# A four-layer hybrid decoder on one core: every projection as a float32r product plus a bf16 product of the rests

## The chip, the cores and the metric

The kernel runs on one core of a Trainium2 chip. The metric is the device time of one execution in microseconds. PE is TensorE (PEld its weight loads), DVE is VectorE, ACT is ScalarE, POOL is GpSimd, and SP is the engine that issues the loads from HBM. PSUM is the memory that PE writes, 8 banks of 512 words per partition; SBUF is the large on-chip memory.

## The reference

```python
D_MODEL, SEQ, DEPTH, D_FF, D_RNN, D_INNER = 1024, 512, 4, 2816, 1280, 2048
for i in range(DEPTH):
    hn = _rmsnorm(x, mix_norm[i])
    mix = (_rg_lru_mixer, _ssd_mixer, _swa_mixer, _hgrn2_mixer)[i](hn, ...)
    x = x + mix
    x = x + _conv_ffn(_rmsnorm(x, ffn_norm[i]), ffn_w_up[i], ffn_conv_w[i], ffn_conv_b[i], ffn_w_down[i])

def _rg_lru_mixer(h, ...):                     # mixer 0, "lru"
    proj = h @ w_in                            # 1024 -> 2 x 1280
    xc = _causal_dwconv(xr, conv_w, conv_b)    # 4 taps
    gates = einsum('bsnc,nce->bsne', xb, w_gate) + b_gate      # ten 128 -> 256 products
    a = exp(-8 * sigmoid(r) * softplus(-lam)); u = sqrt(1 - a * a) * (i * xc)
    hs = scan(a, u); return (gelu(gate_branch) * hs) @ w_out   # 1280 -> 1024

def _ssd_mixer(h, ...):   # mixer 1: h @ w_in (1024 -> 5152), 4-tap convolution, chunked scan, norm, @ w_out (2048 -> 1024)
def _swa_mixer(h, ...):   # mixer 2: h @ w_in (1024 -> 1536), windowed attention with sinks, @ w_out (1024 -> 1024)
def _hgrn2_mixer(h, ...): # mixer 3: h @ w_in (1024 -> 4096), gated linear recurrence, norm, gate, @ w_out (1024 -> 1024)

def _conv_ffn(h, w_up, conv_w, conv_b, w_down):
    u = _causal_dwconv(h @ w_up, conv_w, conv_b)               # 1024 -> 2 x 2816, 3 taps
    return (silu(u[..., D_FF:]) * u[..., :D_FF]) @ w_down      # 2816 -> 1024
```

## The kernel before

Activations lie transposed: 128 features on the partitions, the 512 positions along the free axis, so a projection is made of matmuls of 128x128 weights on 128x512 activations. A *panel* holds the weights of one output tile, `w_panel`, in a ring of 4 (`RING`). It is 1024 words wide for 8 inner tiles, up to 1408 for 11. SP loads the panels in a fixed order, each engine's program is written out by hand, and the engines meet through semaphores: `panel_landed` (the DMA), `panel_split` (POOL's part is made), `panel_used` (PE has finished the panel), `banks_free` (DVE has emptied the PSUM bank), `x_split`, `g_split` and `..._y_split` (the activations are ready in two parts).

float32 is emulated by splitting both operands.

- In the four mixers a value is its upper 16 bits (bf16) and a bf16 remainder. PE reads the upper halves of the weights straight from `w_panel`, and POOL makes `w_lo` (L237). `product` (L291, L292, L293) is three bf16 matmuls: high x high, high x low, low x high. The normalised input is `x_hi` and `x_lo`, the mixer's result `g_hi` and `g_lo`.
- In the FFNs a value is `big` (127/128 of it, rounded to float32r) and `rest` (what is left, in float32r as well). ACT makes `w_big` (L270), then POOL makes `w_rest` (L244). `paired` (L311, L312) is two float32r matmuls: big x big and rest x rest; since `big` is scaled, the two together give the product divided by 128, and the reader of PSUM multiplies it back.

An FFN is done in two halves of the inner width: 12 of the 22 up tiles, the first half of the down projection (`dna`, 8 output tiles of 11 inner tiles), the other up tiles, then `dnb`. `g_big` and `g_rest` are rings of 13 tiles.

Mixer 0 (lines 765 to 874) works in ten units. In a unit DVE takes two projection tiles out of PSUM (L824, L827), applies three taps of the convolution (L840), forms the recurrence (L846 to L850, L860, the scan L862) and splits the result (L874). ACT does the first tap (L781), the gates' tanh, exp and tanh (L765 to L773), the square root (L793) and the high part of the result (L795). Mixer 1 has 41 input tiles in four groups of ten; six tiles of a group go through three taps on DVE (L1268), and in the next group's first tiles the scan's products of the previous group are interleaved. Mixer 2 interleaves 12 tiles with 16 attention units, whose exponentials are ACT's (L1871). Mixer 3 interleaves, for each of 8 heads, eight half tiles with eight levels of its recurrence: PE multiplies (L1470), DVE updates (L1619 to L1622, L1632), PE multiplies again. `residual_scalar` and `residual_vector` take each output tile of a projection into the residual stream and prepare the next norm and its splits, tile by tile.

In the trace the stages are: mixer 0 from 0 to 235.7 us, FFN 0 to 478.4, mixer 1 to 922.8, FFN 1 to 1165.5, mixer 2 to 1422.9, FFN 2 to 1665.6, mixer 3 to 2006, FFN 3 to the end. PE's last stretch in each mixer, in which it does little but the output projection, begins at 187, 880, 1390 and 1960 us.

## Time and profile before

| | before |
|---|---|
| median of 3 runs | 2253.49 us (2251.11 to 2255.06) |
| the profiled execution | 2254.03 us, its span 2252.2 us |
| PE busy | 2075.1 us (92%), 9938 matmuls |
| PE weight loads | 1379.8 us (61%) |
| DVE busy | 1333.1 us (59%) |
| ACT busy | 1060.0 us (47%) |
| POOL busy | 919.6 us (41%) |
| granted TensorE clock, mean | 0.966 |
| chain that ended last | PE 71%, DVE 14%, ACT 10%, issue 3%, DMA 1% |

Matmuls overlap each other, so the busy time of a group of them is more than what they add to the time: their starts tell the pace. A granted clock of 1.0 is 2.4 GHz and 0.5 is 1.2 GHz; means lie between.

### The profile page before, as it was taken

What the parts mean: (1) busy time and instruction counts of PE and PEld (TensorE: products, weight loads), DVE (VectorE), ACT (ScalarE), POOL (GpSimd) and SP (SyncE); (2) the same over time, 40 slices, a digit from 0 to 9 for tenths busy, and PEclk for the clock granted to TensorE, in tenths of its full rate; (3) what the DMA queues carried; (4) which work ended last, traced back from release to release, by engine and by line L of the source; (5) the groups of instructions that cost most, each with busy time, mean ns of one, the idle gap of its engine ahead of it and who ended that gap; (6) DMA issues with size and microseconds to landing.
All of it is one profiled execution on the core that took longest, in us unless ns stands there. A gap on an engine that the chain in (4) does not pass through costs nothing.

```text
span 2252.2 us, 26237 instructions
## 1 busy us (share of the span) xinstructions
PE 2075.1 (92%) x9938; PEld 1379.8 (61%) x9938; DVE 1333.1 (59%) x2011; ACT 1060.0 (47%) x1493; POOL 919.6 (41%) x390
## 2 busy tenths in 40 slices
...
GB/s 157 84 67 59 147 168 115 174 84 65 48 66 66 56 58 93 140 158 131 154 110 57 28 19 38 150 162 123 160 93 66 57 57 57 38 131 156 143 141 122
DMA packets 59165, 225.05 MB, mean 100 GB/s; under 512 B 6688, under 2 KB 7072, under 8 KB 58784
## 3 DMA queue, kind: packets, MB, share of 16 engines
...
## 4 chain that ended last, share of the span: by engine, by line
PE 71%; DVE 14%; ACT 10%; issue 3%; DMA 1%; POOL 0%; SPq 0%; DVEq 0%; ACTq 0%; POOLq 0%
PE psum L311 21%; PE psum L312 21%; PE psum L291 7%; PE psum L292 7%; PE psum L293 7%; DVE arena L1268 3%; PE psum L1470 2%; ACT arena L1871 1%; DVE arena L1943 1%; DVE arena L1948 1%; ACT arena L1155 1%; ACT L447 1%; PE psum L1829 1%; DVE arena L1601 1%; ACT arena L1881 1%
## 5 line engine op out<-in xcount | busy, mean ns | idle before, releaser
L244 POOL TENSOR_TENSOR w_rest<-w_panel,w_big 128x1024 fp32r<-128x1024 f32 (+1 forms) x240 | 626.7, 2632 | 350.0 <-ACT w_big L270 332.9
L237 POOL TENSOR_TENSOR w_lo<-w_panel 128x1024 bf16<-128x1024 f32 (+2 forms) x145 | 288.4, 1989 | 961.1 <-DMA w_panel<-in_ssd_in 243.7
L311 PE MATMUL psum<-x_big,w_big 128*128 128x512 f32 x1408 | 550.3, 391 | 0.0
L312 PE MATMUL psum<-x_rest,w_rest 128*128 128x512 f32 x1408 | 547.9, 389 | 0.0
L291 PE MATMUL psum<-x_hi,w_panel 128*128 128x512 bf16 x840 | 331.4, 395 | 22.9 <-DVE x_lo L420 12.4
L292 PE MATMUL psum<-x_lo,w_panel 128*128 128x512 bf16 x840 | 329.9, 393 | 0.0
L270 ACT ACTIVATE w_big<-w_panel 128x1024 fp32r<-128x1024 f32 (+1 forms) x240 | 263.2, 1132 | 140.5 <-PE psum L312 132.7
L293 PE MATMUL psum<-x_hi,w_lo 128*128 128x512 bf16 x840 | 329.2, 392 | 0.0
L311 PEld LDWEIGHTS psum<-x_big,w_big 128*128 128x128 f32 x1408 | 264.3, 188 | 56.6 <-issue 1.0
L312 PEld LDWEIGHTS psum<-x_rest,w_rest 128*128 128x128 f32 x1408 | 264.3, 188 | 55.7 <-issue 1.0
L312 PE MATMUL psum<-g_rest,w_rest 128*128 128x512 f32 x704 | 278.8, 396 | 0.0
L311 PE MATMUL psum<-g_big,w_big 128*128 128x512 f32 x704 | 278.1, 395 | 0.0
L630 DVE SCALAR_TENSOR_TENSOR psum<-ffn_raw,params,psum 128x512 f32<-128x512 f32 x352 | 264.4, 751 | 6.8
L622 DVE TENSOR_TENSOR ffn_raw<-psum,rstd 128x512 f32<-128x512 f32 x176 | 121.7, 692 | 164.3 <-PE psum L312 147.6
L578 ACT ACTIVATE psum<-ffn_raw,params 128x512 f32<-128x512 f32 x176 | 137.4, 782 | 119.2 <-DVE ffn_raw L622 118.8
L291 PEld LDWEIGHTS psum<-x_hi,w_panel 128*128 128x128 bf16 x840 | 86.8, 103 | 129.2 <-issue 44.9
L437 DVE SCALAR_TENSOR_TENSOR x_resid<-psum,x_resid 128x512 f32<-128x512 f32 x64 | 44.0, 688 | 187.8 <-PE psum L312 187.8
L312 PEld LDWEIGHTS psum<-g_rest,w_rest 128*128 128x128 f32 x704 | 132.1, 188 | 32.5
L311 PEld LDWEIGHTS psum<-g_big,w_big 128*128 128x128 f32 x704 | 132.3, 188 | 31.5
L293 PEld LDWEIGHTS psum<-x_hi,w_lo 128*128 128x128 bf16 x840 | 84.9, 101 | 107.0 <-issue 14.3
L292 PEld LDWEIGHTS psum<-x_lo,w_panel 128*128 128x128 bf16 x840 | 85.1, 101 | 102.7 <-issue 25.1
L291 PE MATMUL psum<-g_hi,w_panel 128*128 128x512 bf16 x336 | 130.7, 389 | 9.5 <-DVE g_lo L874 6.1
...
## 6 DMA issues: line engine op xcount, KB each, us to landing
w_panel<-in_upa SPq DMA_DIRECT2D x96, 512.0 KB, 3.5
w_panel<-in_upb SPq DMA_DIRECT2D x80, 512.0 KB, 3.5
...
w_panel<-in_ssd_in SPq DMA_DIRECT2D x41, 512.0 KB, 3.2
w_panel<-in_hgrn_in SPq DMA_DIRECT2D x32, 512.0 KB, 3.2
w_panel<-in_lru_in SPq DMA_DIRECT2D x19, 512.0 KB, 3.5
w_panel<-in_ssd_out SPq DMA_DIRECT2D x16, 512.0 KB, 3.2
```

Of the source, the lines that this page charges most:

```text
L237: pool.tensor_tensor(k.wl[:, slot, lo:words], raw[:, lo:], k.whi(slot, words)[:, lo:], ALU.subtract).then_inc(k.s("panel_split"), 1)
L244: pool.tensor_tensor(k.w2[:, slot, 0:words], raw, k.w1[:, slot, 0:words].bitcast(F32), ALU.subtract).then_inc(k.s("panel_split"), 1)
L270: act.activation(k.w1[:, slot, 0:words], k.w[:, slot, 0:words], ACT.Copy, scale=(SHIFT - 1) / SHIFT).then_inc(k.s("panel_big"), 1)
L291: pe.matmul(out, wh, ah, start=start, stop=False)
L292: pe.matmul(out, wh, al, start=False, stop=False)
L293: return pe.matmul(out, wl, ah, start=False, stop=stop)
L311: pe.matmul(out, w_big, a_big, start=start, stop=False)
L312: return pe.matmul(out, w_rest, a_rest, start=False, stop=stop)
L578: act.activation(out, k.ffn_raw[:, j % 2, half, 2:], ACT.Identity, bias=k.p("ffn_conv_b", j + (l * 2 * FF_T + half * FF_T)), scale=k.p("ff ...
L622: dve.tensor_tensor(k.ffn_raw[:, j % 2, half, 2:], k.ps[:, k.bank(job, i), :], k.rstd[:, :], ALU.mult).then_inc(k.s("banks_free"), 1)
L630: dve.scalar_tensor_tensor(out, k.ffn_raw[:, j % 2, half, tap:tap + S], k.p("ffn_conv_w", j + ((l * 3 + tap) * 2 * FF_T + half * FF_T)), o ...
L1268: dve.scalar_tensor_tensor(place, b.raw[:, i % 2, tap:tap + S], k.p("ssd_conv_w", tap * 24 + ch), place, ALU.mult, ALU.add).then_inc(k.s(" ...
```

## The change

All projections, those of the mixers too, become one float32r matmul on the big parts (L290 of the new kernel) and one bf16 matmul on the rests (L291). `w_rest`, `x_rest` and `g_rest` are bf16 everywhere, and the scale (`SHIFT`) goes from 128 to 512. ACT rounds every panel (`w_big`), in the mixers too: `round_ahead` stands in ACT's program at chosen places and rounds the panels up to four ahead. POOL takes the rest of every panel. SP reloads a ring slot when its panel is split (`panel_split`) in the mixers as well. All panels are at most 1024 words: the output projections are cut into parts of 5, 7 or 8 inner tiles (`OUT_PARTS`), the first parts of the first output tiles ahead of the others (`out_panel`). The FFN keeps its whole inner width of 22 tiles in `g_big` and `g_rest`, so there is one down projection, and the 8 additions to the residual of `dna` go in each FFN. In mixer 0 the convolution, the square of the decay and the result before its split live in PSUM. Mixer 1's normalised results go through PSUM, mixer 3's result too. In all, 1196 triples of bf16 matmuls and 2112 float32r pairs become 3308 mixed pairs.

```diff
-SHIFT = 128.0
+PANEL = DT * P
+SHIFT = 512.0
+OUT_PARTS = {"lru_out": parts((0, 5, 10)), "ssd_out": parts((0, 8, 16)), "swa_out": parts((0, 8)),
+             "hgrn_out": parts((0, 8))}
+OUT_PARTS.update({f"dn{l}": parts((0, 8, 15, 22)) for l in range(DEPTH)})
+OUT_EARLY = {"lru_out": 2, "ssd_out": 4, "swa_out": 2, "hgrn_out": 4, **{f"dn{l}": 2 for l in range(DEPTH)}}
...
+        self.w1 = sb("w_big", [P, RING, PANEL], F32R)
+        self.w2 = sb("w_rest", [P, RING, PANEL], BF16)
+        self.x1 = sb("x_big", [P, DT, S], F32R)
+        self.x2 = sb("x_rest", [P, DT, S], BF16)
...
+def round_until(act, k, last):
+
+    while k.rounded <= min(last, len(PANELS) - 1):
+        n = k.rounded
+        slot, lo, words = n % RING, PANEL // 2 if n == 0 else 0, PANELS[n][2]
         if n >= RING:
+            act.wait_ge(k.s("panel_used"), n - RING + 1)
+        act.wait_ge(k.s(f"panel_landed{slot}"), 16 * (n // RING + 1))
+        act.activation(k.w1[:, slot, lo:words], k.w[:, slot, lo:words], ACT.Copy, scale=(SHIFT - 1) / SHIFT
+                       ).then_inc(k.s("panel_big"), 1)
+        k.rounded += 1
+
+
+def round_ahead(act, k, job, i):
+
+    round_until(act, k, k.panel0[job] + i + RING)
...
-    pe.matmul(out, wh, ah, start=start, stop=False)
-    pe.matmul(out, wh, al, start=False, stop=False)
-    return pe.matmul(out, wl, ah, start=False, stop=stop)
...
+    pe.matmul(out, w_big, a_big, start=start, stop=False)
+    return pe.matmul(out, w_rest, a_rest, start=False, stop=stop)
...
 def residual_scalar(act, k, c, job):
...
+            last = out_panel(job, o, len(OUT_PARTS[job]) - 1)
+            round_ahead(act, k, job, last - 1)
             act.wait_ge(k.s("banks_free"), k.evicted(job, o))
+            round_ahead(act, k, job, last)
...
+    for k0, k1 in OUT_PARTS[job][:-1] + [(OUT_PARTS[job][-1][0], FF_T - 1), (FF_T - 1, FF_T)]:
+        pe.wait_ge(k.s("g_split"), FF_T * l + k1)
+        for o in range(early):
+            out_steps(pe, k, job, o, k0, k1, k.g1, k.g2)
+    for o in range(early, DT):
+        out_steps(pe, k, job, o, 0, FF_T, k.g1, k.g2)
...
-            act.activation(b.conv[:, u, :], b.raw[:, u, 3:], ACT.Identity, bias=k.p("lru_conv_b", j),
+            act.activation(k.ps[:, conv_bank(u), :], b.raw[:, u, 3:], ACT.Identity, bias=k.p("lru_conv_b", j),
                            scale=k.p("lru_conv_w", j + 3 * LRU_T)).then_inc(k.s("lru_biased"), 1)
...
+            round_ahead(act, k, job, 2 * j + 1)
...
+        act.wait_ge(k.s("lru_decay"), j * 3 + 1)
+        act.activation(k.ps[:, 5, :], b.a, ACT.Square).then_inc(k.s("lru_decay"), 1)
...
-            dve.wait_ge(k.s("lru_decay"), r * 2 + 1)
-            dve.tensor_tensor(b.s, b.a, b.a, ALU.mult).then_inc(k.s("lru_s"), 1)
...
+            dve.wait_ge(k.s("lru_decay"), r * 3 + 3)
+            dve.scalar_tensor_tensor(b.s, k.ps[:, 5, :], 1.0, b.th, ALU.add, ALU.mult).then_inc(k.s("lru_s"), 1)
...
@@ ssd_scalar, conv
                            scale=k.p("ssd_conv_w", 3 * 24 + ch)).then_inc(k.s("ssd_biased"), 1)
+            round_ahead(act, k, "ssd_in", ssd_tile(g, i))
             act.wait_ge(k.s("ssd_tapped"), 3 * ci + 3)
```

The first place is ACT's program in one unit of mixer 0. Before the change it has the first tap (L781), the gates' group (L765 to L773), the two copies for the splits, the square root and the high part.

```order
L779 ACTIVATE arena<-arena 128x512
L781 ACTIVATE arena<-arena,params 128x512
L765 ACT_TABLE_LOAD
L765 ACTIVATE arena<-psum,arena 128x512
L768 ACTIVATE arena<-psum,arena 128x512
L772 ACTIVATE arena<-arena 128x512
L773 ACTIVATE arena<-arena 128x512
L787 ACTIVATE arena<-arena 128x512
L789 ACTIVATE arena<-arena 128x512
L793 ACT_TABLE_LOAD
L793 ACTIVATE arena<-arena 128x512
L795 ACTIVATE g_hi<-arena 128x512
```

In the changed kernel the same stretch of ACT reads so (the gates' group is L722 to L732 now).

```order
L738 ACTIVATE arena<-arena 128x512
L742 ACTIVATE psum<-arena,params 128x512
L237 ACTIVATE w_big<-w_panel 128x1024 x2
L722 ACT_TABLE_LOAD
L722 ACTIVATE arena<-psum,arena 128x512
L725 ACTIVATE arena<-psum,arena 128x512
L729 ACTIVATE arena<-arena 128x512
L730 ACTIVATE arena<-arena 128x512
L732 ACTIVATE psum<-arena 128x512
L755 ACTIVATE arena<-arena 128x512
L757 ACTIVATE lru_conv_big<-psum 128x512
L762 ACT_TABLE_LOAD
```

Two roundings of whole panels now stand between the first tap and the gates' group, and the group has one more member, the square.

The second place is ACT in mixer 1, where the exponentials of the previous group's scan (L1175, L1179) and a tile's convolution (first tap L1155, silu L1158) alternate. Before the change:

```order
L1175 ACTIVATE g_lo<-psum 128x384
L1179 ACTIVATE g_hi<-psum 128x512 x2
L1155 ACTIVATE arena<-arena,params 128x512
L1158 ACT_TABLE_LOAD
L1158 ACTIVATE arena<-arena 128x512
L1187 ACTIVATE x_sq<-arena 128x512
```

In the changed kernel (exponentials L1140 and L1144, first tap L1118, silu L1122):

```order
L1140 ACTIVATE arena<-psum 128x384
L1144 ACTIVATE arena<-psum 128x512 x2
L1118 ACTIVATE arena<-arena,params 128x512
L237 ACTIVATE w_big<-w_panel 128x1024
L1122 ACT_TABLE_LOAD
L1122 ACTIVATE arena<-arena 128x512
L1152 ACTIVATE x_sq<-y_plain 128x512
```

A rounding moves in behind each first tap, ahead of the silu's table load. POOL's subtraction for that panel waited for the panel to land, and now waits for this rounding.

## Rows read from the trace of the kernel before

**Rows 1.** First part of the page: engine, busy us, share, instructions.
```profile
PE 2075.1 (92%) x9938; PEld 1379.8 (61%) x9938; DVE 1333.1 (59%) x2011; ACT 1060.0 (47%) x1493; POOL 919.6 (41%) x390
```

**Rows 2.** Chain of waits, whole run, its shares by line.
```profile
by line: PE psum L311 21.5%; PE psum L312 21.5%; PE psum L291 6.7%; PE psum L292 6.6%; PE psum L293 6.6%; issue 3.2%; DVE arena L1268 3.0%; PE psum L1470 2.3%; ACT arena L1871 1.3%; DVE arena L1943 0.9%; DVE arena L1948 0.8%; ACT arena L115
```

**Rows 3.** Busy time: stretch, us, PE, PEld, DVE, ACT, POOL, clock, DMA share, GB/s.
```profile
25.00:187.00 162.00, 129.24 (x546) 55.10 (x544) 139.09 (x182) 87.84 (x119) 45.46 (x21) 0.92 0.20 65
235.70:478.40 242.70, 242.70 (x1059) 198.50 (x1058) 149.00 (x208) 135.62 (x168) 158.27 (x61) 1.00 0.44 146
880.00:922.80 42.80, 42.80 (x200) 19.39 (x199) 9.90 (x16) 11.39 (x17) 17.81 (x9) 1.00 0.33 111
1230.00:1350.00 120.00, 89.77 (x517) 54.37 (x517) 65.31 (x139) 72.12 (x186) 9.46 (x5) 0.92 0.07 23
1390.00:1422.90 32.90, 32.89 (x155) 14.73 (x152) 13.69 (x21) 14.85 (x23) 11.05 (x6) 1.00 0.34 113
1735.00:1960.00 225.00, 202.97 (x1134) 126.47 (x1132) 119.35 (x261) 60.79 (x73) 44.63 (x23) 0.93 0.15 55
```

**Rows 4.** Timeline of PE in three stretches: start, us, engine, line, operation.
```profile
624.66 0.38 PE L293 MATMUL psum<-x_hi,w_lo 128*128 128x512 bf16 x1
...
628.54 0.38 PE L293 MATMUL psum<-x_hi,w_lo 128*128 128x512 bf16 x1
...
249.62 0.39 PE L311 MATMUL psum<-x_big,w_big 128*128 128x512 f32 x1
...
252.79 0.39 PE L311 MATMUL psum<-x_big,w_big 128*128 128x512 f32 x1
...
1159.69 0.40 PE L311 MATMUL psum<-g_big,w_big 128*128 128x512 f32 x1
...
1165.52 0.40 PE L312 MATMUL psum<-g_rest,w_rest 128*128 128x512 f32 x1
```

**Rows 5.** Groups by form; after the bar busy us, mean ns, idle before.
```profile
L244 POOL TENSOR_TENSOR w_rest<-w_panel,w_big 128x1024 fp32r<-128x1024 f32 x176 | 419.1, 2401 | 297.1 <-ACT w_big L270 280.0 <-PE psum L312 17.1
L237 POOL TENSOR_TENSOR w_lo<-w_panel 128x1024 bf16<-128x1024 f32 x136 | 266.9, 1963 | 890.3 <-DMA w_panel<-in_ssd_in 243.7 <-DMA w_panel<-in_hgrn_in 189.9 <-DMA w_panel<-in_swa_out 144.3
...
L270 ACT ACTIVATE w_big<-w_panel 128x1024 fp32r<-128x1024 f32 x176 | 177.1, 1045 | 71.8 <-PE psum L312 63.9 <-DMA w_panel<-in_upa 7.9
```

**Rows 6.** Chain by line: 187:235.7, 585:672, 805:880, 1735:1960, 1960:2006 us.
```profile
by line: PE psum L291 31.4%; PE psum L292 30.9%; PE psum L293 30.1%; DVE arena L862 2.5%; DVE arena L860 1.4%; DVE arena L870 1.4%; DVE g_lo L874 1.4%; ACT g_hi L795 1.3%; issue 0.4%; DVEq L873 0.0%
...
by line: DVE arena L1268 21.4%; issue 6.8%; PE psum L292 6.0%; PE psum L293 6.0%; PE psum L291 6.0%; DVE arena L1342 5.8%; ACT arena L1155 5.5%; ACT L1175 4.4%; DVE g_hi L1322 4.2%; DVE arena L1339 4.0%; DVE arena L1335 3.2%; PE psum L1059 
...
by line: PE psum L291 19.4%; PE psum L292 19.0%; PE psum L293 18.7%; PE psum L1102 8.1%; PE psum L1092 3.6%; PE psum L1059 3.5%; issue 3.0%; PE psum L1037 2.6%; PE psum L1083 2.4%; PE psum L1080 2.4%; PE psum L1078 2.3%; PE psum L1047 2.3%;
...
by line: PE psum L1470 17.7%; PE psum L293 14.8%; PE psum L291 14.8%; PE psum L292 14.8%; DVE arena L1601 5.6%; issue 4.2%; PE psum L1500 2.5%; PE psum L1508 2.4%; DVE arena L1596 2.2%; DVE arena L1658 2.2%; DVE arena L1622 2.1%; DVE arena 
...
by line: PE psum L291 25.5%; PE psum L292 25.1%; PE psum L293 24.9%; DMA w_panel<-in_hgrn_out 6.8%; POOL w_lo L237 4.1%; PE psum L1508 2.4%; PE psum L1470 2.4%; PE psum L1500 2.2%; PE psum L1503 1.5%; PE psum L1492 1.5%; ACT x_sq L1542 1.3%
```

**Rows 7.** Timeline of DVE, ACT and POOL in one unit of mixer 0.
```profile
88.88 0.68 DVE L824 TENSOR_TENSOR arena<-psum,rstd 128x512 f32<-128x512 f32 x1
...
90.20 0.81 ACT L781 ACTIVATE arena<-arena,params 128x512 f32<-128x512 f32 x1
...
93.08 2.32 POOL L237 TENSOR_TENSOR w_lo<-w_panel 128x1024 bf16<-128x1024 f32 x1 [6.13 <-DMA w_panel<-in_lru_in]
...
94.32 1.63 DVE L846 TENSOR_TENSOR arena<-arena 128x512 f32<-128x512 f32 x1 [0.67 <-ACT arena L772]
...
98.80 2.80 DVE L862 TENSOR_TENSOR_SCAN arena<-arena 128x512 f32<-128x512 f32 x1
```

**Rows 8.** Three lines: duration ns min/median/max, first and last start.
```profile
L870 DVE SCALAR_TENSOR_TENSOR arena<-arena x10: 678/680/2389, 54.6 to 188.6; 128x512 f32<-128x512 f32 x10
...
L1268 DVE SCALAR_TENSOR_TENSOR arena<-arena,params x72: 750/752/2432, 515.9 to 801.5; 128x512 f32<-128x512 f32 x72
...
L1601 DVE TENSOR_TENSOR arena<-arena x8: 683/2380/2382, 1680.4 to 1927.6; 128x512 f32<-128x512 f32 x8
```

More of the change, by code:

```diff
@@ L289, in product, with weights_sync @@
-def product(pe, out, wh, wl, ah, al, start, stop):
-    pe.matmul(out, wh, ah, start=start, stop=False)
-    pe.matmul(out, wh, al, start=False, stop=False)
-    return pe.matmul(out, wl, ah, start=False, stop=stop)
-def gemm_tile(pe, k, bank, slot, kt, hi, lo, k0=0, k1=None, m=P, fresh=None, first=0):
-    wh, wl = k.whi(slot), k.wl[:, slot, :]
-    for q in range(k0, kt if k1 is None else k1):
-        if fresh is not None:
-            pe.wait_ge(k.s("x_split"), DT * fresh + q + 1)
-        a = (q - first) * m
-        last = product(pe, k.ps[0:m, bank, :], wh[:, a:a + m], wl[:, a:a + m],
-                       hi[:, q, :], lo[:, q, :], q == 0, q == kt - 1)
-    return last
+def weights_sync(sp, k, n):
+    job, i, words = PANELS[n]
+    if n >= RING:
+        sp.wait_ge(k.s("panel_split"), n - RING + 1)
+    sp.dma_start(k.w[:, n % RING, 0:words], k.dram[job][i][:, 0:words]).then_inc(k.s(f"panel_landed{n % RING}"), 16)
@@ L402, in residual_vector, with first_vector @@
+def first_vector(dve, k):
+    dve.wait_ge(k.s("gains_landed"), 16)
+    for o in range(DT):
+        dve.wait_ge(k.s(f"x{o}_landed"), 16)
+        if o >= 2:
+            dve.wait_ge(k.s("x_split"), o - 1)
+        dve.tensor_scalar(k.ps[:, 5 + o % 2, :], k.x[:, o, :], gain(k, 0, o), None, ALU.mult
+                          ).then_inc(k.s("x_scaled"), 1)
+        if o == 0:
+            first_rest(dve, k)
+        split_x(dve, k, 0, o)
+        sum_squares(dve, k, 0, o)
 def residual_vector(dve, k, c, job):
@@ L608, in ffn_scalar @@
     if l == DEPTH - 1:
-        for m in range(FFN_PANELS - RING, FFN_PANELS):
-            panel_big(act, k, l, m)
+        round_until(act, k, len(PANELS) - 1)
 def ffn_vector(dve, k, l):
@@ L2028, in _ @@
         def _(pool):
-            for job in jobs:
-                weights_gpsimd(pool, k, job, words[job])
+            for n in range(len(PANELS)):
+                weights_gpsimd(pool, k, n)
+                if n in (3, 5):
+                    gate_weights_gpsimd(pool, k, n // 5)
         @block.tensor
@@ L2082, in panels, with out_panels @@
     return np.stack([np.ascontiguousarray(w[:, :, g].transpose(1, 0, 2)).reshape(P, -1) for g in groups])
+def out_panels(job, w):
+    sizes = out_words(job)
+    out = np.zeros((len(sizes), P, max(sizes)), w.dtype)
+    for part, (k0, k1) in enumerate(OUT_PARTS[job]):
+        rows = panels(w[k0 * P:k1 * P], k1 - k0, [span(o * P) for o in range(DT)])
+        for o in range(DT):
+            out[out_panel(job, o, part), :, 0:rows.shape[2]] = rows[o]
+    return out
 def span(*starts, width=P):
```

670 lines of the change are left out of this document (288 added, 382 removed).

## The prediction

> **What bounds the kernel now.** The page gives PE 92% busy and no other engine more than 59% [rows 1]. That share is an average of stages with different limits, so the chain of waits comes next. Of the span, 43% of the chain lies on the FFN pairs (L311, L312), and 19.9% on the three bf16 products of the mixers' projections (L291 to L293) [rows 2]; 19.9% of 2252.2 is 448 us. The busy time by stretch shows three kinds of stage [rows 3]. An FFN takes 242.7 us, and PE is busy in every one of them. The output projections at the end of the mixers are dense too (42.8 of 42.8, 32.9 of 32.9). Inside the mixers others share the chain: DVE has 139 of 162 us in mixer 0, ACT 72 of 120 in the middle of mixer 2, and PE 203 of 225 in mixer 3. The chain by stretch puts numbers on this [rows 6]: the three products have 92.4% in 187 to 235.7, 18.0% in a group of mixer 1, 57.1% in its last group, 44.4% in mixer 3's six middle heads, 75.5% in its last 46 us.
>
> **The pace of a matmul.** PE's starts tell it [rows 4]. 18 bf16 steps from 624.66 to 628.54 take 215.6 ns each; 14 float32r steps from 249.62 to 252.79 take 226.4 ns; on `g_big` and `g_rest`, 25 steps from 1159.69 to 1165.52 take 233.2 ns. No row alternates the types. Bounds for a mixed pair: two bf16 steps (431 ns) below, two float32r steps (453, on g 466) above. I take one of each, 442 ns (g: 449), since both halves are then as near as a row can be. A triple takes 647 ns, so a projection whose time is PE's alone falls to 0.683 of itself.
>
> The Trainium skill (TensorE: Matmul & The Clock Gate, "Back-to-back issue gap") gives N/2.4 + 2.5 ns, 216 ns for 512 columns, whatever the type. By it the pairs of an FFN are at that pace already, item 1 below is zero, and the sum is -56, 2198 us. The bf16 rows agree with it; the float32r rows are 11 to 18 ns above it, so it has no chance of its own here.
>
> **The change part by part.**
>
> 1. FFNs. 1056 matmuls each stay, 704 on x and 352 on g. A pair on x goes from 453 to 442 ns, on g from 466 to 449: 352 x 0.0108 + 176 x 0.0176 = 6.9 us an FFN, 27 for four. Bounds 0 and 55. The 8 additions for `dna` go at no gain, as they lie beside PE (DVE 149 of 242.7 us). ACT's roundings and POOL's rests are as many words as before.
> 2. Dense ends of the mixers: 45.0 + 42.8 + 32.9 + 0.755 x 46 = 155 us on the chain, minus 0.317 of it: 49 us. Per output tile of 8 pairs PE now needs 3.54 us, ACT one rounding (1.05 [rows 5]) and the three reads of the residual it has now, POOL 2.40: both still fit.
> 3. Last group of mixer 1 (805 to 880): 0.571 x 75 = 42.8 us, times 0.317 = 13.6. The early output steps also cover the exponentials and DVE's multiplication behind them, and a part of that cover is gone: I take 10.
> 4. Mixer 3, middle heads: 0.444 x 225 = 99.9, times 0.317 = 31.7. What is late next is DVE's update between two levels. POOL's op and DVE's cannot both run: L1601 has a minimum of 683 ns and a median of 2380 [rows 8]. POOL's op grows from 1.96 to 2.40 us [rows 5] (its inputs are then the same as in an FFN; bounds 1.96 and 2.40, the inputs decide), and two stand back to back behind each place where ACT rounds two panels. A head has two such places; DVE misses up to 4.8 us at each, most of it beside its present idle time (it is busy 119 of 225). I take 3 us a head, 18 in six, of bounds 0 and 6 x 5.
> 5. The rest of the 448 us, 448 - 155 - 43 - 100 = 150, is spread over mixers 1, 2 and the first heads of mixer 3, with 18% of the chain in a group [rows 6]. The full share is 48; where DVE's and ACT's chains run beside PE only half comes through, 24.
> 6. Mixer 0's units are not PE's. One unit: DVE takes the tiles out at 88.88, ACT's first tap starts at 90.20, and the gates' group follows it until the scan at 98.80 [rows 7]. Two roundings stand between now, 2 x 1.05, and the square, at most as long as the first tap's 0.81, say 0.6: 2.7 us a unit on the way to the scan. Against it, DVE no longer runs into POOL: a collision made L846 1.63 us, and L870 has 2389 at most against 680 [rows 7, 8]. That the convolution now lies in PSUM, and that POOL's operations fall into the time in which DVE waits for the gates, I take to spare 1.3 us a unit (bounds 0 and the 2.6 of two collisions like L846's and the scan's). Nine units took 134 us (L870's starts), 14.9 each: I expect 16.3, so +13. The gates' weights are rounded in unit 0 (2560 words of ACT) and the start gets a multiplication per x tile on DVE: +3. Bounds for all of it 0 and 30.
> 7. Mixer 1's convolution. The three taps (L1268) have a median of 752 and a maximum of 2432 ns, and take 21% of a group's chain [rows 6, 8]. The rounding ends about 1 us after the taps begin, so POOL starts in the middle of them each time, where now it comes with the panel's landing. 24 convolved tiles x 0.5 us: +12; bounds 0 and 24 x 1.6.
> 8. Mixer 2: six of its twelve roundings stand in the stretch where ACT is on the chain: +6 [rows 3].
> 9. Seven transitions between a mixer and an FFN. PE's cover for the last x tile shrinks from 7 triples to 7 pairs or stays, and ACT has a rounding ahead of its copy: +1 us each, +7.
>
> Sum: -27 - 49 - 10 - 31.7 + 18 - 24 + 13 + 3 + 12 + 6 + 7 = -83. The profiled execution took 2254.0, 0.5 above the median of 2253.5, so I predict 2171. SP's earlier reload of a slot I cost at nothing: the loads take 0.2 of the DMA's time in the mixers [rows 3] and POOL's wait for them is idle time off the chain. The wider PSUM use of the mixers' results is at nothing too, since DVE does the same number of operations there; without that cover it would be some 0.7 us a tile.
>
> **The rivals.**
>
> A. *Only the chain counts.* All 448 us shrink by 0.317 (142) and the FFNs give 27, with no new cost: 2085. For it: PE is 92% busy, and ACT (47%) and POOL (41%) have room on the average. Against it: in mixer 0 ACT's new work is in series with DVE by the order of instructions. Chance 0.15.
>
> B. *The mixers' insides give nothing.* Items 3, 4 and 5 come out at zero, since DVE and ACT close the gap that PE leaves, and the added items stay: 2254 - 27 - 49 + 13 + 3 + 6 + 7 = 2207, and 12 more with the taps, 2219. For it: in a group of mixer 1 DVE's taps alone have more of the chain (21.4%) than the three products (18.0%) [rows 6], with ACT's steps in series. Chance 0.17.
>
> C. *Slower: POOL shuts DVE out.* Place: the 105 input panels of the mixers. Each of POOL's operations now starts when ACT lets it, among DVE's own steps, and holds DVE for its full 2.40 us instead of now and then. At 2 us more each that is +210, in place of the 30 of items 4 and 7: 2171 - 30 + 210 = 2351. It decides from (83 + 30) / 105 = 1.1 us a panel. For it: L1601's median. Against it: DVE has idle time at these places, and an operation with an operand in PSUM shows no such spread (mixer 0's taps move there). Chance 0.07.
>
> The Trainium skill (SBUF — State Buffer, "Who interferes with whom") calls the pair of ports that DVE shares with GpSimd an exclusive lock, taken by a DVE instruction with two SBUF inputs; the trace agrees (683 against 2380 ns).
>
> My forecast, 0.61: its own range is 2125 to 2215. That the change removes the matmuls is certain from the order of instructions, so there is no case in which it does nothing.
>
> **How the numbers follow.** 0.2% of the time, 4.5 us, is about what a measurement can tell from no change. A and the forecast end faster, B too in nearly all of its range. Slower is C, with the upper edge of B: 0.08; same 0.01; faster 0.91. The range takes half of A and most of B and the bounds of items 1, 4 and 7: 2095 to 2232.
>
> **What would show it.** In an FFN, PE's steps alternate and 16 of them take 3.54 us, the stage 236; with 3.45 the float32r surcharge was a matter of the pair and is gone, with 3.62 it is paid by both. In mixer 0, starts of the unit's last product of DVE 16.3 us apart, ACT's roundings between tap and tanh, PE half idle. In mixer 3, a head takes 35 us or less; if it is still 37.5, B is right. In mixer 1, the maxima of the taps move from some to nearly all third taps. The dense ends are some 34, 29, 23 and 35 us long. I would be wrong mostly through items 4, 5 and 7, where PE, DVE and ACT are close to each other, or if a mixed pair costs more than 453 ns, which no row here excludes: 10 ns more on 3308 pairs is up to 33 us.

## The result: slower by 0.56%

The changed kernel takes 2263.98 us, median of 5 runs (2263.68 to 2267.62), against 2252.94 for the kernel before (median of 5, 2250.32 to 2255.06): ratio 1.0056, 95% interval 1.0041 to 1.0071. I had predicted 2171, with 0.08 for slower.

Its page, first part, beside [rows 1]:

```profile
PE 1924.9 (85%) x8742; PEld 971.7 (43%) x8742; DVE 1307.7 (58%) x1977; ACT 1225.8 (54%) x1715; POOL 996.0 (44%) x431
```

PE is busy for 150 us less, and the kernel takes 11 us more. By stage, in us of the profiled executions; a mixer is cut where DVE ends its last step on the mixer's output (`g_lo` before, `y_rest` after; what comes then is output projection alone), and an FFN starts at its first matmul. The middle column is the kernel before without its third product (experiment 3):

| stage | before | third product left out | after |
|---|---|---|---|
| mixer 0, inside + end | 182.8 + 44.9 | 183.6 + 31.2 | 193.6 + 33.2 |
| mixer 1 | 392.7 + 51.7 | 367.2 + 36.4 | 405.1 + 37.1 |
| mixer 2 | 225.1 + 32.3 | 221.9 + 23.1 | 234.8 + 23.0 |
| mixer 3 | 311.4 + 28.9 | 280.2 + 22.8 | 306.9 + 22.8 |
| FFN 0, 1, 2, 3 (first to last matmul) | 242.7 each | 242.7 to 242.9 | 244.8, 244.8, 253.6, 254.1 |

The ends lose 41.7 us, nearly as much as with the removal alone (44.3). Inside the mixers the removal gives 59 us, while the changed kernel takes 28 more than the kernel before.

Busy time by stretch (columns as in [rows 3]); mixer 0, FFN 0, FFN 2, middle of mixer 3:

```profile
25.00:195.00 170.00, 112.00 (x376) 48.15 (x376) 113.78 (x175) 117.50 (x157) 59.16 (x26) 0.83 0.19 64
...
234.40:479.20 244.80, 244.17 (x1059) 109.74 (x1059) 136.68 (x201) 143.53 (x186) 158.46 (x70) 1.00 0.42 145
...
1423.90:1677.50 253.60, 247.04 (x1059) 110.17 (x1058) 139.56 (x205) 148.19 (x193) 160.66 (x70) 0.98 0.40 141
1740.00:1965.00 225.00, 178.78 (x973) 120.35 (x972) 147.98 (x264) 85.58 (x101) 60.37 (x24) 0.88 0.18 59
```

Three things are to be seen. An FFN is longer with PE busy throughout. FFN 2 is 8.8 us longer still, with PE idle for 6.6. And in the middle of mixer 3 PE did 24 us less than in [rows 3], while DVE did 29 us more, with nearly the same number of instructions (264 and 261).

**The pair.** PE and its weight loads in FFN 2, and the loads' groups:

```profile
1499.57 0.58 PE L290 MATMUL psum<-x_big,w_big 128*128 128x512 f32 x1
1499.99 0.39 PE L291 MATMUL psum<-x_rest,w_rest 128*128 128x512 bf16 x1
1500.03 0.58 PE L290 MATMUL psum<-x_big,w_big 128*128 128x512 f32 x1
```
```profile
L290 PEld LDWEIGHTS psum<-x_big,w_big 128*128 128x128 f32 x2240 | 464.8, 207 | 73.1 <-DVE x_rest L402 28.7 <-POOL w_rest L251 21.4 <-issue 15.3
L291 PEld LDWEIGHTS psum<-x_rest,w_rest 128*128 128x128 bf16 x2240 | 218.9, 98 | 593.4 <-issue 587.7
```

A pair on x takes 0.46 us, above both bounds that I had (431 and 453 ns); on g it takes 0.46 as well, just under the 466 of two float32r steps there. Ahead of each bf16 weight load the profile shows 0.26 us of idle "issue" time (587.7 / 2240); the float32r loads have hardly any.

**The hold.** DVE, ACT and POOL at one convolved tile of mixer 1, and two lines of DVE in mixers 1 and 3 (durations in ns, min/median/max):

```profile
605.01 0.81 ACT L1118 ACTIVATE y_plain<-arena,params 128x512 f32<-128x512 f32 x1 [1.47 <-DVE arena L1229]
605.73 1.04 ACT L237 ACTIVATE w_big<-w_panel 128x1024 fp32r<-128x1024 f32 x1
605.86 4.32 DVE L1238 SCALAR_TENSOR_TENSOR y_plain<-arena,params,y_plain 128x512 f32<-128x512 f32 x3 [0.88 <-ACT y_plain L1118]
...
606.85 2.78 POOL L251 TENSOR_TENSOR w_rest<-w_panel,w_big 128x1024 bf16<-128x1024 f32 x1 [9.75 <-ACT w_big L237]
...
610.22 0.63 ACT L1122 ACTIVATE y_plain<-y_plain 128x512 f32<-128x512 f32 x1 [2.14 <-DVE y_plain L1238]
```
```profile
L1238 DVE SCALAR_TENSOR_TENSOR y_plain<-arena,params,y_plain x48: 750/752/2756, 524.3 to 815.6; 128x512 f32<-128x512 f32 x48
...
L1597 DVE TENSOR_TENSOR arena<-arena x56: 410/420/2612, 1696.0 to 1968.3; 128x256 f32<-128x256 f32 x56
```

Three taps take 4.32 us in place of 3 x 0.75. ACT's rounding ends one us into them, POOL starts, and one tap stands still until about the time POOL has ended. Of the 72 taps (48 write `y_plain`, the others `arena`), 24 are held, one in each of the 24 convolved tiles, 47 us in all; in the kernel before, where POOL started when a panel landed, it was 18 of 72 and 24 us.

**The loop at a mixer's end.** End of mixer 2, the last tile of the residual:

```profile
1431.11 0.69 DVE L434 SCALAR_TENSOR_TENSOR x_resid<-psum,x_resid 128x512 f32<-128x512 f32 x1
...
1431.82 1.06 ACT L237 ACTIVATE w_big<-w_panel 128x1024 fp32r<-128x1024 f32 x1 [1.47 <-DVE x_resid L434]
1432.79 0.71 ACT L359 ACTIVATE x_big<-x_resid,shifted_gain 128x512 fp32r<-128x512 f32 x1
...
1433.40 0.67 ACT L363 ACTIVATE psum<-x_resid,params 128x512 f32<-128x512 f32 x1
...
1434.17 0.69 DVE L402 SCALAR_TENSOR_TENSOR x_rest<-x_big,psum 128x512 bf16<-128x512 f32 x1 [2.38 <-ACT psum L363]
1434.78 0.68 DVE L394 TENSOR_TENSOR x_sqsum<-x_sq,psum 128x512 f32<-128x512 f32 x1
...
1434.91 0.79 PE L290 MATMUL psum<-x_big,w_big 128*128 128x512 f32 x1 [3.02 <-DVE x_rest L402]
```

Addition, rounding, two copies, split, sum of squares, next addition: the additions of mixer 2's end stand 4.27 us apart (the first two 3.73, the last two start at 1426.84 and 1431.11), and a tile of 8 pairs needs PE for 3.68. PE had ended the eighth tile at 1424, so the additions are 7 us behind, and FFN 2's first panel, which wants every x tile, waits for them: 3.53 and 3.02 us. The matmul at 1434.91 takes 0.79 us where 0.58 is usual; PE ran at half clock, as the stretch from 1430 to 1439 shows:

```profile
1430.00:1439.00 9.00, 5.33 (x10) 2.14 (x11) 3.09 (x6) 5.51 (x8) 3.40 (x2) 0.50 0.34 117
```

Before, ACT had no rounding in this loop, and a tile of 8 triples needed PE for 5.18 us, which hid it. Mixers 0 and 1 have 10 and 16 pairs a tile, 4.6 and 7.4 us, and FFN 0 and 1 start without loss.

### The profile page after: what moved, and what is told of

Its sections match the earlier page's. It is cut to its first block, busy times and chain, and to the rows that moved or that the text cites. A ratio compares the mean times of both kernels' runs of the same rounds, so it can differ in the third digit from the quotient of the medians.

```text
span 2264.9 us, 23882 instructions
## 1 busy us (share of the span) xinstructions
PE 1924.9 (85%) x8742; PEld 971.7 (43%) x8742; DVE 1307.7 (58%) x1977; ACT 1225.8 (54%) x1715; POOL 996.0 (44%) x431
## 4 chain that ended last, share of the span: by engine, by line
PE 61%; DVE 19%; ACT 14%; issue 5%; DMA 1%; POOL 0%; DVEq 0%; ACTq 0%; SPq 0%
PE psum L291 26%; PE psum L290 26%; PE psum L1445 3%; DVE y_plain L1238 3%; ACT w_big L237 2%; ACT arena L1846 1%; DVE arena L1597 1%; PE psum L1802 1%; DVE arena L1599 1%; DVE arena L1596 1%; DVE arena L1918 1%; DVE arena L1923 1%; DVE arena L1238 1%; ACT L443 1%; ACT L440 1%
## 5 line engine op out<-in xcount | busy, mean ns | idle before, releaser
L251 POOL TENSOR_TENSOR w_rest<-w_panel,w_big 128x1024 bf16<-128x1024 f32 (+3 forms) x425 | 989.6, 2342 | 1249.4 <-ACT w_big L237 1249.4
L290 PE MATMUL psum<-x_big,w_big 128*128 128x512 f32 x2248 | 1096.9, 597 | 51.6 <-DVE x_rest L402 32.7
L291 PE MATMUL psum<-x_rest,w_rest 128*128 128x512 bf16 x2248 | 900.5, 401 | 0.0
L237 ACT ACTIVATE w_big<-w_panel 128x1024 fp32r<-128x1024 f32 (+3 forms) x425 | 421.2, 1017 | 222.5 <-DVE x_resid L434 124.2
L290 PEld LDWEIGHTS psum<-x_big,w_big 128*128 128x128 f32 x2248 | 466.1, 207 | 74.9 <-DVE x_rest L402 29.9
L291 PEld LDWEIGHTS psum<-x_rest,w_rest 128*128 128x128 bf16 x2248 | 219.8, 98 | 593.7 <-issue 587.7
L290 PE MATMUL psum<-g_big,w_big 128*128 128x512 f32 x704 | 324.3, 578 | 0.0
L291 PE MATMUL psum<-g_rest,w_rest 128*128 128x512 bf16 x704 | 274.0, 389 | 0.0
L290 PE MATMUL psum<-y_big,w_big 128*128 128x512 f32 x336 | 168.1, 605 | 21.5 <-DVE y_rest L841 9.3
L291 PEld LDWEIGHTS psum<-g_rest,w_rest 128*128 128x128 bf16 x704 | 67.1, 95 | 178.8 <-issue 178.8
L290 PEld LDWEIGHTS psum<-g_big,w_big 128*128 128x128 f32 x704 | 141.0, 200 | 0.0
L291 PE MATMUL psum<-y_rest,w_rest 128*128 128x512 bf16 x336 | 137.2, 408 | 0.0
L1445 PE MATMUL psum<-arena 128*128 128x64 f32 (+1 forms) x512 | 75.1, 295 | 56.1 <-DVE arena L1599 55.2
```

Source lines behind the costliest of these rows:

```text
L237: act.activation(k.w1[:, slot, lo:words], k.w[:, slot, lo:words], ACT.Copy, scale=(SHIFT - 1) / SHIFT).then_inc(k.s("panel_big"), 1)
L251: pool.tensor_tensor(k.w2[:, slot, lo:words], k.w[:, slot, lo:words], k.w1[:, slot, lo:words].bitcast(F32), ALU.subtract).then_inc(k.s("pa ...
L290: pe.matmul(out, w_big, a_big, start=start, stop=False)
L291: return pe.matmul(out, w_rest, a_rest, start=False, stop=stop)
L1445: mm = pe.matmul(out, b.ks[:, h % 2, chunk[c]], rhs, start=True, stop=True)
```

## The experiments

Each is an edit of the changed kernel, where it doesn't say "before". A plus or minus behind a time is against the changed kernel's 2263.98 where no other kernel is named, and in experiments 2, 3 and 10 against the kernel before. Mixers are given in us, in order, each from its first matmul (in experiment 10 as in the table); by that measure mixer 2 is 256.6 in the changed kernel, the others as in the table.

**1. Matmuls by type** (e1_grouped).

```
-    for q in range(k0, k1):
-        mm = paired(pe, out, k.w1[:, slot, a], k.w2[:, slot, a], k.x1[:, q, :], k.x2[:, q, :], ...)
+    for rest in (False, True):
+        for q in range(k0, k1):
+            w, x = (k.w2, k.x2) if rest else (k.w1, k.x1)
+            mm = pe.matmul(out, w[:, slot, a], x[:, q, :], ...)
```

The output projections are edited alike. In a stage's first panel the float32r products wait for `x_hi` only, the bf16 ones for `x_split`.

> The changed kernel, with the matmuls of a panel in another order: first all float32r products of the panel (or of the piece of it that is run in one go), then all bf16 products of the rests. The same matmuls, the same operands. Theory P (the price lies in the change of type: in the changed kernel a pair takes 460 ns, PE's weight loads of the bf16 half show 0.25 us of idle time each, so they are not pulled ahead under a float32r matmul): the pair falls to 442 ns on x (the two steps that the kernel before showed, 226 and 216), an FFN from 244.8 to about 236, four FFNs -36 us, and the dense ends of the mixers -4: about 2224. Rival Q (each of the two types has its price in this mix, whatever its neighbour): the pair stays at 460 and the time at 2264.

Measured 2240.25, ratio to the kernel before 0.9945 (0.993 to 0.996). FFN 0 is 238.9 long, FFN 2 249.1. The bf16 loads' idle time:

```profile
L307 PEld LDWEIGHTS psum<-x_rest,w_rest 128*128 128x128 bf16 x2248 | 195.0, 100 | 287.9 <-issue 108.9 <-DVE x_rest L409 1.2
```

P holds in kind: 587.7 us of "issue" become 108.9. The gain is 24 us where 36 to 40 was expected. A panel of 8 pairs on x takes 3.58 us, against 3.68 in the changed kernel and the 3.54 of P: the bf16 steps take 216 ns, but the float32r steps some 231 (225 to 236) and not 226.

**2. Mixed pairs alone in the kernel before** (e2_before_ffn_mixed).

```
-        self.w2 = sb("w_rest", [P, RING, PANEL], F32R)
+        self.w2 = sb("w_rest", [P, RING, PANEL], BF16)   # likewise x_rest and g_rest
```

> The kernel before, with w_rest, x_rest and g_rest as bf16 instead of float32r, in the FFNs alone; the mixers keep their three bf16 products. It does the part of the change that lies in item 1 of the prediction. Theory P: pairs on x go from 453 to 460 ns, pairs on g from 466 to 460: 1408 x 0.007 - 704 x 0.006 = +6 us, 2259. Rival (item 1 as predicted, the loss of the changed FFNs comes from elsewhere): -27, 2226.

Measured 2258.39, ratio 1.0021 (1.0008 to 1.0035): +6, as P has it. My item 1 had the wrong sign.

**3. The third product left out of the kernel before** (e3_before_two).

```
     pe.matmul(out, wh, ah, start=start, stop=False)
-    pe.matmul(out, wh, al, start=False, stop=False)
-    return pe.matmul(out, wl, ah, start=False, stop=stop)
+    return pe.matmul(out, wh, al, start=False, stop=stop)
```

> The kernel before, with the third bf16 product of the mixers' projections (the rests of the weights times the upper halves of the activations) left out; all else stays, POOL's subtractions too. It tells what the removal of a third of these matmuls is worth by itself, with none of the change's new work. By the prediction (items 2 to 5 without the added 18 us, at the whole 0.333 of the chain's shares): about -120, 2133. Theory K (a sparser PE is clocked down, and the chains of DVE and ACT close the gap): only the dense ends give, 155 x 0.333 = -52, and the insides of the mixers next to nothing: about 2195, with the granted clock inside the mixers lower than in the kernel before.

Measured 2153.84, ratio 0.9562 (0.9545 to 0.9579): -99 by the medians. The profiled executions are 103 apart, of which the ends give 44 and the insides 59 by the spans of the table. Two stretches inside mixers 0 and 3:

```profile
25.00:175.00 150.00, 90.20 (x340) 36.69 (x344) 135.54 (x173) 79.41 (x109) 45.38 (x22) 0.83 0.22 70
...
1660.00:1870.00 210.00, 173.67 (x967) 115.19 (x986) 130.04 (x268) 62.39 (x76) 45.89 (x24) 0.91 0.19 58
```

The granted clock did fall (0.83 from 0.92 in [rows 3]), and the time was gained all the same. K is out: the removal is worth 99 us, and the change gives them back elsewhere. What the insides would give at the full clock, this run doesn't tell.

**4. The rounding behind the three reads** (e4_late_round).

```
             act.wait_ge(k.s("banks_free"), k.evicted(job, o))
-            round_ahead(act, k, job, last)
         ... the three activations on k.x[:, o, :] ...
+        if job is not None:
+            round_ahead(act, k, job, last)
```

> The changed kernel, with one of ACT's steps moved: in the loop over the eight tiles of the residual at a mixer's or an FFN's end, the rounding of the panel that takes the slot of the tile's last panel stands behind the three reads of the residual instead of ahead of them. Theory L (at the ends of mixers 2 and 3 that rounding of 1.06 us is in a loop with DVE's addition, ACT's copies and DVE's split, 4.27 us a tile against PE's 3.68; PE waits in it, and is at half clock at the start of FFN 2 and FFN 3): the loop falls to some 3.7 us a tile, the two ends lose 4 us each and FFN 2 and FFN 3 return from 254 to 245: -18 to -26, about 2242. Rival M (a later rounding makes POOL's rest late by as much, and PE waits for it instead): the time stays within 4 us of 2264.

Measured 2245.14, ratio 0.997 (0.9959 to 0.9982): -19, L holds but for the ends. The end of mixer 2 and FFN 2:

```profile
1390.00:1421.30 31.30, 29.71 (x142) 15.66 (x145) 13.78 (x24) 22.82 (x39) 14.34 (x6) 0.95 0.27 84
1421.30:1665.30 244.00, 244.00 (x1040) 109.18 (x1060) 137.09 (x202) 144.06 (x186) 157.78 (x69) 1.00 0.44 143
```

The additions are 3.33 us apart now, and FFN 2 is 244.0 long with PE at 1.00, against 253.6 at 0.98. The ends stayed at 23.0 and 23.7: the loop had not lengthened them, it was paid behind them.

**5. POOL's subtraction on 8 words** (e5_tiny_pool).

```
+    if n >= RING and PANELS[n][0][:2] not in ("up", "dn"):
+        words = lo + 8
     pool.wait_ge(k.s("panel_big"), n + 2)
```

> The changed kernel, with POOL's subtraction for the mixers' panels (all but the first four) on 8 words of each partition instead of 640 to 1024, so most of the rests are left out; the count of operations and all waits stay. It takes away POOL's 2.4 us and what they hold up. The mixers of the changed kernel are 226.8, 442.1, 256.6 and 329.7 us; with the third product merely left out of the kernel before they are 215, 403, 244 and 303: the new work costs 91 us there. Theory H (DVE is held while POOL runs: in mixer 3 the six heads have 47.8 us of DVE time above each instruction's shortest, against 19.9 before; in mixer 1's two groups 28 against 24): mixer 3 gives back 25, mixer 1 10, mixers 0 and 2 together 5, and the rests come sooner behind ACT's roundings (2): about -42, 2222. Rival R (the rounding on ACT is what costs): within 10 us of 2264.

Measured 2152.68, ratio 0.9562 (0.9547 to 0.9577): -111, more than twice what H named. (The edit reaches 101 of the mixers' 105 input panels and their 48 output panels; the ends moved by at most 1.3 us, so I put it down to the 101.) Mixers 226.2, 378.6, 254.2, 284.1: it is mixers 1 (-63.5) and 3 (-45.6). The same lines of DVE as above:

```profile
L1240 DVE SCALAR_TENSOR_TENSOR y_plain<-arena,params,y_plain x48: 750/752/754, 518.3 to 756.0; 128x512 f32<-128x512 f32 x48
...
L1599 DVE TENSOR_TENSOR arena<-arena x56: 410/419/422, 1629.0 to 1856.0; 128x256 f32<-128x256 f32 x56
```

The maxima of 2756 and 2612 ns are gone, with the waits left as they were. The durations of DVE's instructions add up to 62 us less in mixer 1 (312.8 to 250.9) and 53 less in mixer 3 (221.4 to 168.3), and the stages follow.

**6. ACT's rounding on 8 words** (e6_tiny_act): the same edit at the rounding.

> The changed kernel, with ACT's rounding of the mixers' panels (all but the first four) on 8 words of each partition, so the big part of most weights is left out; the count of operations, all waits and POOL's whole subtraction stay. It takes away 1.05 us a panel on ACT. Theory R (ACT's roundings stand in series with its steps for DVE: 2 x 1.05 a unit in mixer 0, by the gates; six in mixer 2's middle; 32 convolved or gate tiles in mixer 1, where the next panel's rounding stands ahead of the first tap's wait): mixer 0 -15, mixer 1 -25, mixer 2 -6, mixer 3 -8, and the output projections of mixers 2 and 3 with the starts of FFN 2 and 3 behind them -20: about -74, 2190. Theory H (POOL's lock is the larger part): -25, almost all of it at the output projections and FFN 2 and 3, with the mixers' insides unchanged.

Measured 2234.68, ratio 0.9925 (0.9908 to 0.9942): -29. The size is H's, the place is not: H left the insides unchanged, and they gave most of it. Mixer 0 -14.0, mixer 2 -9.6 and mixer 3 -6.6 are near what R said; mixer 1 +1.6 is where R fell (-25), and FFN 2 gave 3.8 and FFN 3 nothing.

**7. Both edits that gained** (e7_grouped_late).

> The changed kernel with both edits that gained alone: the matmuls of a panel by type, and the late rounding in the residual's loop. Alone they gave -24 and -19 on 2264. If their gains are apart (the one in PE's pairs, the other in the loop between DVE and ACT): -43, 2221, 1.4% below the kernel before. If a faster PE meets the same loop, less than the sum: in the grouped run alone FFN 2 and FFN 3 kept 10 us of start-up loss each (249 against 239), which the late rounding should take away whole; so 2221 again, and with a remainder of the loop 2230.

Measured 2222.87, ratio 0.987 (0.9855 to 0.9886): -41, nearly the sum. The four FFNs are 237.9 to 239.1 long, FFN 2 and 3 as short as the others.

**8. A third product again** (e8_third).

```
     pe.matmul(out, w_big, a_big, ...)
+    pe.matmul(out, w_rest, a_rest, start=False, stop=False)      # mixers only
     pe.matmul(out, w_rest, a_rest, ...)
```

> The changed kernel with a third matmul for each pair of the mixers' projections: the bf16 product of the rests is added twice (an extra term, so the result is off by it). 1208 matmuls of 216 ns more, the PE work of the kernel before. Theory N (PE's share of the chain was real, and the new work on DVE, ACT and POOL ate the gain): the time goes up by about the 99 us that leaving the third product out of the kernel before gave, less what now hides beside the new work: +60 to +100, 2325 to 2365, and the granted clock inside the mixers returns to 0.92 to 0.95. Theory K (the gain was lost because a sparser PE is clocked down): +0 to +25, 2264 to 2290, with the same return of the clock.

Measured 2340.8, ratio 1.0396 (1.0381 to 1.0412): +77, N (the matmuls added are 1176, 254 us of PE). The mixers take 87 us more, and FFN 2 and 3 take 8.8 and 4.5 less: with three matmuls for a pair, PE's time for a tile seems to cover the residual's loop again, in part for FFN 3. Inside mixer 0 nothing moves (163.5 to 163.3 until the output projection) while the granted clock goes from 0.83 to 0.91. So there neither PE's work nor its clock is in the chain, unless the two cancel:

```profile
25.00:195.00 170.00, 138.46 (x543) 59.43 (x543) 113.83 (x175) 117.13 (x157) 59.18 (x26) 0.91 0.21 64
```

**9. The rests of mixers 1 and 3 by DVE** (e9_rests_by_dve), on top of 7.

```
+def weights_vector(dve, k, job, i):
+    dve.wait_ge(k.s("panel_big"), n + 2)
+    dve.tensor_tensor(k.w2[:, slot, :], k.w[:, slot, :], k.w1[:, slot, :].bitcast(F32), ALU.subtract
+                      ).then_inc(k.s("panel_split"), 1)
     def conv(g, i):                                    # and at four of the eight halves of a head
+        weights_vector(dve, k, job, ssd_tile(g, i) + 3)
         dve.wait_ge(k.s("panel_used"), k.used(job, ssd_tile(g, i)))
```

POOL passes over these panels.

> The kernel of the two edits that gained (matmuls by type, late rounding: 2223), with the subtraction that makes the rests moved from POOL to DVE for the input panels of mixer 1 (37 of 41) and mixer 3 (28 of 32). DVE does each just before it next waits for PE, one projection later than the panel's rounding. POOL's subtraction costs the changed kernel 63.5 us in mixer 1 and 45.6 in mixer 3 (from the run with it on 8 words). A subtraction of 1024 words on DVE is estimated at 1.2 us, from the 0.68 of 512 words. Theory H (while POOL's 2.4 us run, a DVE instruction with both inputs in SBUF stands still, so that DVE pays for POOL's work in full): DVE pays 37 x 1.2 = 45 in mixer 1 and 34 in mixer 3 instead, part of it in time in which it waits for PE anyway: -20 to -45 us, 2178 to 2203. Rival (DVE is the bound there, and work of its own is dearer than being held now and then): 2223 or slower.

Measured 2147.88, ratio 0.9536 (0.9522 to 0.9551): -75 on kernel 7, beyond the range that H gave, and the fastest of all. Mixer 1 goes from 445.1 to 418.0, mixer 3 from 328.7 to 284.5.

```profile
L268 DVE TENSOR_TENSOR w_rest<-w_panel,w_big x65: 1211/1218/1225, 502.5 to 1817.5; 128x1024 bf16<-128x1024 f32 x65
...
L1264 DVE SCALAR_TENSOR_TENSOR y_plain<-arena,params,y_plain x48: 750/752/754, 515.1 to 783.1; 128x512 f32<-128x512 f32 x48
```

The same subtraction takes DVE 1.22 us. With POOL doing it, DVE lost up to 2 us of its own. In mixer 3 the 34 us of new work cost nothing: the stage is as short as with POOL's subtractions cut to 8 words (284.1). They stand just ahead of DVE's waits for PE, which I take for the reason.

**10. POOL on 8 words in the kernel before** (e10_before_tiny_pool).

```
-            pool.tensor_tensor(k.wl[:, slot, lo:words], raw[:, lo:], ...
+            hi = words if n < RING or job == "lru_out" else lo + 8
+            pool.tensor_tensor(k.wl[:, slot, lo:hi], raw[:, lo:hi], ...
```

> The kernel before, with POOL's subtraction for the mixers' panels on 8 words of each partition (all but the first four and mixer 0's output panels), so most of the lower halves of the weights are left out. In the changed kernel the same cut gave 111 us. Theory G (the hold grew with the change: there each subtraction starts right behind ACT's rounding, among DVE's taps and updates, and takes 2.40 us, where here it comes when the panel lands and takes 1.96, and PE's third product covers much of it): -30 to -60, 2190 to 2220. Rival S (DVE was held by as much before, and the change added little to it): -85 to -111, 2140 to 2165.

Measured 2177.26, ratio 0.9664 (0.9648 to 0.968): -74, between G and S. Mixers 212.5, 406.2, 258.5, 316.1. So the hold was there already, and the change moved it from (15, 38, -1, 24) us in the four mixers to (1, 63, 2, 46): +36 in all. In mixer 1 DVE's durations fall by 50 us here (300.7 to 250.5) and by 62 in experiment 5. So DVE stands still for only 12 us more there, and it costs 25: of that time 47 us now fall on the taps, and 24 before, and the taps have the largest share of the chain in that mixer's group [rows 6].

**11. POOL's subtraction on 13 of 16 words** (e11_pool_shorter).

```
+        words = words * 13 // 16
```

> The changed kernel, with POOL's subtraction for the mixers' panels (all but the first four) on 13 of 16 words, so that it takes about 1.95 us for 1024 words instead of 2.40: the time it took in the kernel before, at the place where it stands now. The last 3 of 16 rests are left out. If the 111 us that POOL costs here are in step with its duration: -0.19 x 111 = -21, 2243. If what counts is where it starts (every collision once, whatever its length) less: -10. If the short version falls through the gaps between DVE's instructions: more than -40.

POOL in mixer 1 before the change, after it, and in this run:

```profile
L237 POOL TENSOR_TENSOR w_lo<-w_panel 128x1024 bf16<-128x1024 f32 x48 | 94.3, 1964 | 311.8 <-DMA w_panel<-in_ssd_in 243.7 <-DMA w_panel<-in_ssd_out 64.9 <-PE psum L312 3.2
...
L251 POOL TENSOR_TENSOR w_rest<-w_panel,w_big 128x1024 bf16<-128x1024 f32 x47 | 121.0, 2576 | 280.2 <-ACT w_big L237 280.2
...
L253 POOL TENSOR_TENSOR w_rest<-w_panel,w_big 128x832 bf16<-128x832 f32 x47 | 101.8, 2168 | 285.4 <-ACT w_big L237 285.4
```

Measured 2240.72, ratio 0.9949 (0.9934 to 0.9964): -23, a little more than in step: the subtraction is 16% shorter (2.58 to 2.17 us in mixer 1, 2.52 to 2.12 in mixer 3) and 21% of the 111 us are back. Mixer 1 -12.2, mixer 3 -13.6. The run takes back two thirds of the lengthening, which was 0.61 and 0.57 us (from 1.96 and 1.95), not the 0.44 that I had. Scaled to the whole of it, an estimate, the longer subtraction explains 18 and 19 of the 25 and 21 us of growth there; the rest, 7 and 2, may be where it starts, which was not tried by itself.

**12. Mixer 0's roundings behind the gates** (e12_round_behind_gates), on top of 9.

```
-            round_ahead(act, k, job, 2 * j + 1)         # behind the first tap, for j > 0
+        if j and conv:
+            round_ahead(act, k, job, 2 * j + 1)         # ahead of the square root
```

> The kernel with the rests of mixers 1 and 3 on DVE, and in mixer 0 ACT's two roundings of a unit moved behind the gates' activations, the tanh and the copy of the convolution (ahead of the square root). With ACT's roundings on 8 words mixer 0 fell from 226.8 to 212.8 us. Theory (the roundings' cost there is their place between the tap and the gates): mixer 0 gets 10 to 14 us back, and all else stays. Rival (they are as much in the way at the new place, ahead of the root on which DVE waits, or POOL's subtractions now fall on the scan): 0 to +5.

Measured 2161.67, ratio 0.9598 (0.9584 to 0.9612): +14 on kernel 9, mixer 0 226.0 to 238.8. My theory fell, and both reasons of the rival are to be seen, though it gave 5 us at most, and POOL falls on the instruction ahead of the scan. One unit, ACT, POOL and DVE:

```profile
107.76 0.58 ACT L781 ACTIVATE lru_conv_big<-psum 128x512 fp32r<-128x512 f32 x1
...
108.23 2.00 ACT L237 ACTIVATE w_big<-w_panel 128x1024 fp32r<-128x1024 f32 x2
...
109.36 4.70 POOL L251 TENSOR_TENSOR w_rest<-w_panel,w_big 128x1024 bf16<-128x1024 f32 x2 [12.97 <-ACT w_big L237]
...
111.54 0.63 ACT L788 ACTIVATE arena<-arena 128x512 f32<-128x512 f32 x1
...
112.28 2.33 DVE L853 SCALAR_TENSOR_TENSOR arena<-arena 128x512 f32<-128x512 f32 x1 [3.05 <-ACT arena L788]
```

The roundings delay the root, on which DVE waits 3.05 us, and POOL, now late too, holds the next DVE instruction with both inputs in SBUF for 2.33 us, where its like (L870 in [rows 8]) takes 0.68. Where the change had put them, POOL runs under taps with an operand in PSUM (see the last paragraph of the next section).

## Why the prediction was wrong

**What PE gives up (items 2 to 5, -115 without the new costs).** Nearly right: the removal alone is worth 99 (experiment 3), and adding as much again costs 77 (experiment 8; 87 in the mixers). The views of the chain by stretch did tell this. Rival A was wrong in taking the change for the removal alone, and B in taking nothing for the insides.

**Item 1 (-27) failed, and it is the largest single miss.** It took one step of each kind, each from a row where it stood beside its own kind. The pair is 460 ns and each FFN 2.1 us longer, +8 in four; experiment 2 shows +6 of it by itself. I had named this way of being wrong, and given it no case of its own. The price is in the alternation: by type, -24.

**Item 2 (-49) near, its "both still fit" wrong.** The ends lost 41.7. But I compared each engine's own sum with PE's 3.54 us a tile, and not the loop that runs through DVE and ACT in turn, 4.27 us. Its lag came due at the start of FFN 2 and 3: 6.5 us of waiting and some 2 us for a stretch at half clock in FFN 2, as much again in FFN 3, +19 for both (experiment 4). My transitions (item 9) had 2 for these two.

**Items 3 to 5, the insides.** -66 by my shares, +18 in item 4 and +12 in item 7 for the hold. The removal alone gives 59 (experiment 3), so the shares held; what was new took it all and 28 us more.

**Items 4 and 7, the hold, mis-sized.** The mechanism was named, with its place: "DVE misses up to 4.8 us at each, most of it beside its present idle time", and "POOL starts in the middle of them each time". Item 4's term came out near, +21 (24 to 46) where I had +18, but not its reason: of the 53 us that DVE stands still in mixer 3, 46 reach the time, so little of it lies beside idle time. Item 7 is what failed in size: I took 0.5 us a tile against 1.0 measured (taps held: 24.3 us before, 47.4 after), +25 for a term of +12. In both, POOL's subtraction is 2.5 to 2.6 us long and not 2.40. I also took the hold of the kernel before for a matter of a few collisions; it was 74 us, a third of them in mixer 3's updates. Rival C had the mechanism and the size of the whole (+210 at 2 us a panel; measured 111 for 101 input panels, 1.1 us each, 74 of it old), but its point of decision, 1.1 us of *new* time a panel, was not reached.

**Item 6 (+16) near.** The inside of mixer 0 grew by 10.8 us. ACT's roundings cost mixer 0 14.0 us (experiment 6), where 2.1 us in nine units would be 19, and the spared collisions are worth 14.6 (15.2 before, 0.6 after), where 1.3 in nine units would be 12; the square was not measured by itself. Units went from 14.8 to 15.3 us (DVE's starts, nine units), not to 16.3. **Item 8 (+6)** measured 9.6.

**The sum as measured.** Removal -99; hold +36; ACT's roundings in mixers 0, 2 and 3, at most 30; mixed pairs +8 in the FFNs; FFN 2 and 3's start +19. That is -6, and the change gave +11. Of the 17 missing, mixed pairs in the mixers are worth some 13 by estimate: experiment 3 ran two bf16 steps of 431 ns and the change 460, on 1196 pairs, of which 0.38 counts (99 us gained of the 258 us taken from PE). The terms were each measured alone and needn't add up exactly; 4 us stay open. Beside the forecast, the same terms read:

| term | forecast | measured |
|---|---|---|
| mixed pairs in the FFNs (item 1) | -27 | +8 |
| matmuls removed, with the pair's price (items 2 to 5) | -115 | -99 + 13 by estimate |
| the hold (items 4 and 7, less 1.3 us a unit in item 6) | +18 | +36 |
| start of FFN 2 and 3 (item 9) | +2 | +19 |
| ACT's new work in the mixers (items 6 and 8) | +33 | at most +30 |
| the other transitions (item 9) | +5 | not measured by itself |

Of the 94 us between the two sums, the two rows on the mixed pair and the removal hold 64, and the hold and the loop 35; the rest is within what the last two rows leave open.

**The clock.** A lower granted clock in the mixers did not eat the gain: experiment 3 has it too and is 99 us faster, and in mixer 0 a higher one brought nothing (experiment 8). It counted where PE is the bound again right after a wait, at the start of FFN 2 and 3, by some 2 us each.

**The hold and PSUM.** Mixer 0's taps, which now have an operand in PSUM, show none of it in the changed kernel:

```profile
L811 DVE SCALAR_TENSOR_TENSOR psum<-arena,params,psum x30: 743/756/756, 40.0 to 179.3; 128x512 f32<-128x512 f32 x30
...
98.10 2.33 DVE L811 SCALAR_TENSOR_TENSOR psum<-arena,params,psum 128x512 f32<-128x512 f32 x3
98.80 4.68 POOL L251 TENSOR_TENSOR w_rest<-w_panel,w_big 128x1024 bf16<-128x1024 f32 x2 [11.37 <-ACT w_big L237]
```

POOL is at work through the whole of 21 of the 30 taps, and none takes more than 756 ns.

The Trainium skill (SBUF — State Buffer, "Who interferes with whom") has DVE and GpSimd share a pair of ports under an exclusive lock, taken by a DVE instruction with two SBUF inputs. The trace agrees: 756 ns at most here, 2756 in mixer 1, where both inputs are in SBUF.
